# Later places for the last gate/up block, another unit order for the mixer's output product, and query transposes inside the query product

## What is computed

```python
# first block
h = rms_norm(x, mix_norm_g)
x = x + concat(y_pool, y_dn) @ w_mix_out          # y_dn: gated delta net, 8 heads of 128
q = (rms_norm(x, xa_norm_g) @ w_xq)               # 4 heads of 512
k, v = split(rms_norm(mem, mem_norm_g) @ w_xkv)
x = x + softmax(q @ k.T * 512**-0.5) @ v @ w_xo
x = x + (silu(causal_dwconv(h @ w_gate)) * (h @ w_up)) @ w_down     # width 5632
# second block
...
f = square(relu(h @ w_up)) @ w_down               # width 8192
# beside both: mod = silu(c) @ w_ada + b_ada, 24 pieces of 512 columns
```

## Time and profile before

| | |
|---|---|
| median of 3 runs | 2915.92 us (2914.46 to 2915.98) |
| the profiled execution's own time | 2910.81 us |
| its span | 2909.0 us |
| TensorE busy | 2801.5 us, 96% of the span |
| DVE, ACT busy | 1768.6 us (61%), 1313.5 us (45%) |
| mean granted clock of TensorE | 0.978 |
| chain that ended last, share by engine | PE 93%, DVE 4%, ACT 2%, issue 1% |

### The profile page before, as it was taken

The page is one execution under the profiler, slowest core; times in us unless marked ns, Lnnn a source line. Parts: engine busy times, 40 slices in busy tenths (PEclk is TensorE's granted clock), DMA queues, the critical chain, the costliest instruction groups (busy, mean ns, idle before and its releaser), DMA issues.

```text
span 2909.0 us, 35765 instructions
## 1 busy us (share of the span) xinstructions
PE 2801.5 (96%) x13510; PEld 2383.5 (82%) x13510; DVE 1768.6 (61%) x2028; ACT 1313.5 (45%) x1658; POOL 172.1 (6%) x132
## 2 busy tenths in 40 slices
PE   8998989999999999999999989998989999999998
PEld 8998968888878888788888889876778787887886
DVE  4466557776557887765555564454774655744445
ACT  5454234454434545434444454344454344344443
POOL 0001620000000000000000002630000000000000
PEclk9999989999999999999999999998999999999999
DMA  8453028887647777775555556450555765855553
GB/s 281 149 173 115 1 103 284 279 279 266 234 148 253 276 275 263 274 253 195 192 183 203 188 181 201 162 185 1 170 194 186 263 219 204 275 190 172 194 185 122
DMA packets 293265, 579.59 MB, mean 199 GB/s; under 512 B 9168, under 2 KB 46192, under 8 KB 292112
## 3 DMA queue, kind: packets, MB, share of 16 engines
q1 hardware_dynamic: 291296, 566.08, 57.6%
q0 software_dynamic: 1120, 8.57, 0.8%
q10 hardware_dynamic: 720, 3.15, 0.3%
HBM read 575.66 MB, written 2.10 MB: 199 GB/s over the span
## 4 chain that ended last, share of the span: by engine, by line
PE 93%; DVE 4%; ACT 2%; issue 1%; DMA 0%; POOL 0%; DVEq 0%; SPq 0%; ACTq 0%
PE GP L866 28%; PE GP L868 27%; PE GP L867 27%; PE TA L842 2%; PE TB L473 2%; PE TB L842 1%; PE GP L459 1%; PE TB L885 1%; PE TA L1213 1%; DVE wlo L1749 0%; DVE ada_acc L1737 0%; DVE small L550 0%; PE TA L1069 0%; PE GP L1069 0%; PE GP L1059 0%
## 5 line engine op out<-in xcount | busy, mean ns | idle before, releaser
L1749 DVE TENSOR_TENSOR wlo<-raw,whi 128x1024 fp32r<-128x1024 f32 (+2 forms) x904 | 1082.1, 1213 | 777.7 <-ACT whi L1289 766.1
L1289 ACT CAST whi<-raw 128x1024 fp32r<-128x1024 f32 (+2 forms) x904 | 920.7, 1029 | 1152.4 <-PE GP L868 1065.6
L866 PE MATMUL GP<-whi,hhi 128*128 128x512 f32 (+2 forms) x1792 | 691.6, 386 | 9.8 <-DVE wlo L1749 6.7
L867 PE MATMUL GP<-wlo,hhi 128*128 128x512 f32 (+2 forms) x1792 | 683.2, 381 | 0.0
L868 PE MATMUL GP<-whi,hlo 128*128 128x512 f32 (+2 forms) x1792 | 683.1, 381 | 0.0
L866 PEld LDWEIGHTS GP<-whi,hhi 128*128 128x128 f32 x1792 | 340.0, 190 | 62.1 <-issue 10.0
L868 PEld LDWEIGHTS GP<-whi,hlo 128*128 128x128 f32 x1792 | 339.4, 189 | 52.6
L867 PEld LDWEIGHTS GP<-wlo,hhi 128*128 128x128 f32 x1792 | 339.7, 190 | 51.6 <-issue 1.0
L866 PE MATMUL GP<-whi,bhi 128*128 128x512 f32 x704 | 276.7, 393 | 0.2 <-DVE blo L1809 0.2
L1737 DVE SCALAR_TENSOR_TENSOR ada_acc<-raw,csig,ada_acc 128x512 f32<-128x512 f32 x360 | 270.2, 750 | 10.2
L868 PE MATMUL GP<-whi,blo 128*128 128x512 f32 x704 | 274.4, 390 | 0.0
(11 more groups left out here) (413 smaller groups left out, 2660.1 us busy)
## 6 DMA issues: line engine op xcount, KB each, us to landing
raw<-in_w_up SPq DMA_DIRECT2D x108, 1024.0 KB, 5.4
raw<-in_w_down SPq DMA_DIRECT2D x108, 1024.0 KB, 5.1
raw<-in_w_ada SPq DMA_DIRECT2D x96, 1024.0 KB, 5.2
raw<-in_w_gate SPq DMA_DIRECT2D x44, 1024.0 KB, 5.2
raw<-in_w_in SPq DMA_DIRECT2D x48, 856.0 KB, 4.7
raw<-in_w_xkv SPq DMA_DIRECT2D x32, 1024.0 KB, 5.6
raw<-in_w_in SPq DMA_DIRECT2D x24, 1024.0 KB, 4.9
raw<-in_w_in SPq DMA_DIRECT2D x24, 864.0 KB, 4.6
```

The lines of the kernel that those rows point to most:

```text
L866: pe.matmul(o, ahi[:, kt, t], whi[r][:, k, 0:q.width], start=first, stop=False)
L867: pe.matmul(o, ahi[:, kt, t], wlo[r][:, k, 0:q.width], start=False, stop=False)
L1289: nc.scalar.copy(whi[(2 * g + s) % NRING][:, :, 0:q.width], raw[j % NSLOT][:, 2 * s:2 * s + 2, 0:q.width])\
L1749: TTo(wlo[r][:, :, 0:q.width], raw[j % NSLOT][:, 2 * s:2 * s + 2, 0:q.width], whi[r][:, :, 0:q.width].bitcast(F32), ALU.subtract).then_inc ...
```

## The change

1. **Gate/up.** The steps on the last block leave the hook ahead of the next third unit and go behind it (hook 3 of the next iteration, or of the following down product for the last iteration), on ACT and DVE, in `ffn1a`, `ffn1b` and `up20` to `up23`. To have a first iteration that differs, `down1a`, `ffn1b` and the `up2`/`down2` phases are written out with `head`. In `down22` they stand ahead of `gate_column` and `gate_copy`, which are in the same hook.
2. **`mix_out`.** The list of units becomes (block, unit) = 00, 01, 10, 11, 02, 03, 12, 13, and the four "a" loads stand behind the last four units. `rank` is a unit's place in it and takes the place of b * units + u. `out_upper` and the subtraction (`out_lower`) go behind the split of the fourth unit.
3. **Queries.** Three of the four groups are transposed inside `xq`, after its seventh, eleventh and fifteenth unit, all through `TA`; ACT copies each after it has split two more units. The fourth stays behind the product and no longer waits for `ada_read`.

```diff
+        if name == "mix_out":
+            g.sort(key=lambda x: (x[2] // 2, x[1], x[2]))
+        self.rank = {x[1:]: i for i, x in enumerate(g)}
         for i, x in enumerate(g):
             self.seq.append(x)
-            if ada and name == "ffn1a":
-                if 2 <= i < 6:
-                    self.seq.append(("a", 0, i - 2))
+            if ada and name in ("ffn1a", "mix_out"):
+                if 0 <= i - (4 if name == "mix_out" else 2) < 4:
+                    self.seq.append(("a", 0, i - (4 if name == "mix_out" else 2)))
...
-            return q.sub0 + it * q.subs + (b + 1) * 2 * q.units
+            return q.sub0 + it * q.subs + (q.rank[b, q.units - 1] + 1) * 2
...
+                    for b, u in q.rank:
+                        if u == 0:
+                            pe.wait_ge(S(f"evac{b % 2}"), it * (q.nb // 2) + (q.ev0 + b // 2 + 1))
+                        if b == 0:
+                            pe.wait_ge(*ready(u))
+                        for s in range(2):
+                            pos = q.seq.index(("g", b, u))
+
+                            pe.wait_ge(S("unit_used"), it * (2 * len(q.seq)) + 2 * (q.unit0 + pos) + s + 1 + CREDIT)
+                            r = (q.rank[b, u] * 2 + s) % NRING
...
+            def query_turn(g):
+                pe.wait_ge(S(f"evac{g % 2}"), 2 + PH["xq"].ev0 + g // 2)
+                if g == 0:
+                    pe.wait_ge(S("kx_c"), 8)
+                else:
+                    pe.wait_ge(*N("qx", "c", g))
+                for f in range(4):
+                    for h in range(NH):
+                        c = (4 * g + f) * P
+                        m = turn(TA[:, f * T + h * P:f * T + h * P + P], kv[:, h, c:c + P])
+                m.then_inc(N("qx", "t")[0], 1)
+
             product(PH["xq"], hhi, hlo, lambda u: (S("norm_lo"), 16 + 2 * u + 2),
-                    first=lambda: pe.wait_ge(S("norm_lo"), 24), points={unit_of(k): lambda k=k: key_turn(k) for k in range(4)})
-            for e in range(2):
-                pe.wait_ge(S(f"evac{e}"), 1 + PH["xq"].ev1)
-            pe.wait_ge(S("ada_read"), 1 + PH["xq"].ada1)
-            pe.wait_ge(S("kx_c"), 8)
-            turn_in(pe, turn, "qx", kv, 0, 0)
+                    first=lambda: pe.wait_ge(S("norm_lo"), 24), points={unit_of(k): lambda k=k: key_turn(k) for k in range(4)} |
+                    {unit_of(v_): lambda g=g: query_turn(g) for g, v_ in enumerate((6, 10, 14))})
+            query_turn(3)
...
-            out_upper(0)
-            out_upper(1)
...
+            phase(PH["mix_out"], hooked({3: lambda: (out_upper(0), out_upper(1)), 6: lambda: raw_square(1, (0,)), 7: lambda: raw_square(1, (1,)), 11: lambda: raw_root(1)},
...
+            def query_copy(g):
+                act.wait_ge(*N("qx", "t", g + 1))
+                nc.scalar.copy(qTx[:, 4 * g:4 * g + 4, :], v(TA, T)).then_inc(N("qx", "c")[0], 1)
+
+            phase(PH["xq"], hooked({2 + k: lambda k=k: key_copy(k) for k in range(4)} | {v_ + 2: lambda g=g: query_copy(g) for g, v_ in enumerate((6, 10, 14))},
+                                   store(PH["xq"], kv, scale=2)), peel=True)
+            query_copy(3)
...
-                return {q.units + LEAD: [evac(0)], 2 * q.units: [gate], 2 * q.units + LEAD: [evac(1), up]}
-
-            phase(PH["ffn1a"], ffn1(PH["ffn1a"], 0), head={3: [lambda it: raw_square(3)],
-                                                           4: [lambda it: (raw_upper(3, 6), raw_upper(3, 7), raw_root(3))]})
-            phase(PH["down1a"], {})
-            phase(PH["ffn1b"], ffn1(PH["ffn1b"], 6))
+                return {3: [lambda it: None if isinstance(it, int) and it == 0 else up(it - 1)], q.units + LEAD: [evac(0)],
+                        2 * q.units: [gate], 2 * q.units + LEAD: [evac(1)]}, lambda it: up(q.n - 1)
+
+            hooks, rest = ffn1(PH["ffn1a"], 0)
+            phase(PH["ffn1a"], hooks, head={3: [lambda it: raw_square(3)], 4: [lambda it: (raw_upper(3, 6), raw_upper(3, 7), raw_root(3))]})
+            phase(PH["down1a"], {}, head={3: [rest]})
+            hooks, rest = ffn1(PH["ffn1b"], 6)
+            phase(PH["ffn1b"], hooks, head={3: []})
...
-                return {q.units + LEAD: [evac(0)], 2 * q.units: [square(0)], 2 * q.units + LEAD: [evac(1), square(1)]}
+                return {3: [lambda it: it and square(1)(it - 1)], q.units + LEAD: [evac(0)], 2 * q.units: [square(0)],
+                        2 * q.units + LEAD: [evac(1)]}, square(1)
...
+                hooks, rest = up2(PH[f"up2{s}"], s)
+                phase(PH[f"up2{s}"], hooks, head={3: [] if s else [lambda it: (second_upper(1, 6), second_upper(1, 7))]})
+                last = [lambda it, rest=rest: it or rest(1)]
+                phase(PH[f"down2{s}"], {3: last + [lambda it: it and post_block(1, 1)], 7: [lambda it: post_block(1, 2 * it)],
                                         8: [lambda it: root_table() if it else None]} if s == 3 else {},
-                      peel=(s == 3), head={3 + i: [lambda it, i=i: gate_copy(1, i)] for i in range(4)} if s == 2 else {})
+                      peel=(s == 3), head=joined({3: last} if s < 3 else {}, {3 + i: [lambda it, i=i: gate_copy(1, i)] for i in range(4)} if s == 2 else {}))
...
-                return {(b + 1) * q.units + LEAD: [hook(b)] for b in range(q.nb)}
+                return {q.rank[b, q.units - 1] + 1 + LEAD: [hook(b)] for b in range(q.nb)}
...
-            for hf in range(NH):
-                t = slice(hf * P, hf * P + P)
-                dve.wait_ge(S("dn_hi"), hf + 1)
-                TTo(hlo[:, 8:16, t], AB[0][hf], hhi[:, 8:16, t].bitcast(F32), ALU.subtract).then_inc(S("dn_lo"), 1)
-
-            phase(PH["mix_out"], hooked({9: lambda: raw_mean(1), 12: lambda: raw_scale(1)},
+            def out_lower():
+                for hf in range(NH):
+                    t = slice(hf * P, hf * P + P)
+                    dve.wait_ge(S("dn_hi"), hf + 1)
+                    TTo(hlo[:, 8:16, t], AB[0][hf], hhi[:, 8:16, t].bitcast(F32), ALU.subtract).then_inc(S("dn_lo"), 1)
+
+            phase(PH["mix_out"], hooked({3: out_lower, 9: lambda: raw_mean(1), 12: lambda: raw_scale(1)},
...
-                return {2 * q.units: [gate], 2 * q.units + LEAD: [up]}
-
-            phase(PH["ffn1a"], ffn1(PH["ffn1a"], 0), links=2,
+                return {3: [lambda it: None if isinstance(it, int) and it == 0 else up(it - 1)], 2 * q.units: [gate]}, lambda it: up(q.n - 1)
+
+            hooks, rest = ffn1(PH["ffn1a"], 0)
+            phase(PH["ffn1a"], hooks, links=2,
                   head={3: [lambda it: raw_mean(3)], 4: [lambda it: (raw_lower(3, 6), raw_lower(3, 7), raw_scale(3))]})
-            phase(PH["down1a"], add_to_x(PH["down1a"]))
-            phase(PH["ffn1b"], ffn1(PH["ffn1b"], 6), links=2)
+            phase(PH["down1a"], add_to_x(PH["down1a"]), head={3: [rest]})
+            hooks, rest = ffn1(PH["ffn1b"], 6)
+            phase(PH["ffn1b"], hooks, links=2, head={3: []})
...
-                return {2 * q.units: [low(0)], 2 * q.units + LEAD: [low(1)]}
+                return {3: [lambda it: it and low(1)(it - 1)], 2 * q.units: [low(0)]}, low(1)
...
-                    hooks |= {4: [lambda it: it and gated(1, 1)], 8: [lambda it: gated(1, 2 * it)]}
-                phase(PH[f"down2{s}"], hooks, peel=(s == 3), head={3 + i: [lambda it, i=i: gate_column(1, 80, i)] for i in range(4)} if s == 2 else {})
+                    hooks |= {3: last, 4: [lambda it: it and gated(1, 1)], 8: [lambda it: gated(1, 2 * it)]}
+                head = {3 + i: [lambda it, i=i: gate_column(1, 80, i)] for i in range(4)} if s == 2 else {}
+                if s < 3:
+                    head[3] = last + head.get(3, [])
+                phase(PH[f"down2{s}"], hooks, peel=(s == 3), head=head)
             post_mean(1)
             TTo(o3[:, 0, c3], o3[:, 0, c3], gpb[1][:, c3], ALU.mult)
```

More of the change, by code:

```diff
@@ new lines, in iteration @@
+                    for b, u in q.rank:
[7 more added lines that the diff above has]
+                            r = (q.rank[b, u] * 2 + s) % NRING
+                            for k in range(2):
+                                kt = u * UK + 2 * s + k
+                                first, last = kt == 0, kt == q.units * UK - 1
+                                for h in range(NH):
+                                    t = slice(h * P, h * P + P)
+                                    o = GP[:, 2 * (b % 2) + h, 0:q.width]
+                                    pe.matmul(o, ahi[:, kt, t], whi[r][:, k, 0:q.width], start=first, stop=False)
+                                    pe.matmul(o, ahi[:, kt, t], wlo[r][:, k, 0:q.width], start=False, stop=False)
+                                    m = pe.matmul(o, alo[:, kt, t], whi[r][:, k, 0:q.width], start=False, stop=last)
+                            m.then_inc(S("mm_done"), 1)
+                        if mid and b % 2 == 1 and u == 1:
+                            mid(it)
+                        if late and b == 0 and u == 0:
```

(11 more changed lines are left out.)

53 lines of the change are left out of this document (5 added, 48 removed).

## The result

The changed kernel takes **2890.03 us**, the median of 4 runs (2889.56 to 2892.27), beside 2915.95 us (2914.46 to 2916.55) for the kernel before on the same chip: 25.9 us less, a ratio of 0.991 with a 95% interval of 0.9896 to 0.9923. The forecast was 2893.4 us, so 3.4 us of the gain were not in it, and the time lies at the lower end of the range.

What follows compares the result with a forecast made beforehand. TensorE bounds the kernel, busy 2801.5 of 2909.0 us, so only its idle time and the half clock behind stalls could be gained. 12.1 + 1.4 + 8.3 + 0.7 = 22.5 us off 2915.9 gave 2893.4 us, range 2890 to 2901.

Steps and rivals of the forecast that it cites:

- the 1.6 us wait for `dg`: In down22 TensorE waits up to 1.6 us for dg; 1.4 us to be gained, 0.6 as lower bound.
- rival 4: Inner iteration boundaries: moved steps ahead of the fourth unit cause 13 stalls of 4 us, giving 2945; chance 0.03.
- rival 2: Crowded "a" loads in mix_out: TensorE stalls once per iteration, 4 us each, giving 2901.4; chance 0.1.
- Rival 3: Three down products: the wait only moves, as something else holds the third unit, giving 2901.6; chance 0.07.
- the price of `down1a`, `down20`, `down21`: Stalls of 2.66, 2.18 and 2.48 us go, with 1.6 us of half clock each: 12.1 us gained.
- the queries: Score products start 3.4 us earlier, three groups inside xq add 2.65: net 0.7 us gained, between 1.0 gained and 0.9 lost.
- rival 1: Half clock in the score products, all else as forecast: 1.6 us more, 2895.0; chance 0.2.
- an idle time of 1.88 us was not followed by one: Query part: that idle time brought no half clock, one of 2.18 did; used to weigh half clock in the score products.
- the step from the profiled execution to the median: Whole kernel: the median lies 5.1 us above the profiled 2910.8, so 22.5 is taken from 2915.9.
- `mix_out`'s term: In mix_out the 6.72 us stall and 1.6 of half clock go: 8.3 us gained, between 6.7 and 8.4.
- its spread of 1.5 us: Run-to-run spread of the whole kernel, 2914.5 to 2916.0, allowed for in the lower end of the range, 2890.

Runs made afterwards that it cites:

- e8: Kernel before with the four "a" loads of down1a, down20 and down21 put behind the third to sixth unit, last block unmoved; 2902.51 us, ratio 0.9958.
- e9: Kernel before, its order kept, with unused matmuls filling TensorE's four stalls (27 in mix_out, 11, 9 and 10 in down1a, down20, down21); 2906.09 us, ratio 0.9974.
- e7: Kernel after plus ten unused matmuls in the two idle times ahead of the score products (six and four); 2889.15 us, ratio 0.9916 to the kernel before.
- e4: Kernel before with only the query part: three of the four groups transposed inside xq; 2916.84 us, ratio 1.0009.
- e6: Kernel after with its query part undone, all four groups behind the product again; 2890.43 us, ratio 0.9913 to the kernel before.
- the two looks: Two more profiled executions of the unchanged kernel before; 2916.11 and 2917.21 us.
- e1: Kernel before, run and profiled again without edit; 2915.39 us, median of 11 runs, ratio 0.9997; profiled at 2910.6 us.
- e2: Kernel before with only the gate/up part: the last block's steps moved behind the third unit; 2898.45 us, ratio 0.9942.
- e3: Kernel before with only the mix_out part: units and "a" loads reordered, hhi and hlo steps behind the fourth unit's split; 2902.27 us, ratio 0.9959.
- e11: Kernel before, unchanged, profiled once more as the first of two further looks; execution of 2916.11 us.
- e12: Kernel before, unchanged, profiled once more as the second of two further looks; execution of 2917.21 us.
- e5: Kernel after, unchanged, run again on a second chip beside the kernel before; 2891.22 us, ratio 0.992.
- e10: Kernel after with unused matmuls in five idle times of TensorE: 6, 4, 17, 33 and 49; 2885.26 us, ratio 0.9898 to the kernel before.

## Why the prediction was right and wrong

The program is cut here at matmuls that are the same in every trace (the first of a product or of its second iteration, or the first behind transposes); us between them, the forecast's change last. `down1a` and `down20` are first iterations; their second ones are in the row below each:

| stretch | before, 2910.8 | before, 2916.1 | after, 2889.6 | forecast |
|---|---|---|---|---|
| start to `mix_out` | 402.59 | 401.56 | 402.21 | |
| `mix_out` | 105.56 | 103.96 | 94.45 | -8.3 |
| `xkva`, `xkvb` | 181.63 | 181.63 | 181.63 | |
| `xq`, attention | 139.62 | 142.57 | 142.00 | -0.7 |
| `xo`, `ffn1a` | 369.81 | 369.73 | 369.83 | |
| `down1a` | 71.40 | 71.69 | 67.09 | -4.3 |
| `ffn1b` | 298.34 | 298.32 | 298.34 | |
| `down1b` to `w_in2b` | 252.16 | 252.68 | 253.09 | |
| first matmuls of 31 columns | 27.37 | 29.03 | 29.00 | |
| on to `down20` | 414.09 | 416.79 | 413.92 | |
| `down20` | 43.08 | 43.08 | 39.03 | -3.8 |
| on to `down21` | 140.54 | 140.53 | 140.53 | |
| `down21`, `up22` | 183.94 | 183.92 | 179.56 | -4.1 |
| `down22` to the end | 278.87 | 278.81 | 277.12 | -1.4 |
| span | 2909.0 | 2914.3 | 2887.8 | -22.5 |

**Right: where the time goes.** The four stalls and the 1.6 us wait for `dg` are gone, the clock is 1.00 behind them, and nothing took their place at the inner boundaries (rival 4: `ffn1a` and `ffn1b` take what they took) or in `mix_out`'s second half (rival 2: no wait, at 364 GB/s). Rival 3 falls too: with the queue of two steps gone, no `wlo` is late in any of the three, and e8 got nearly there by moving the "a" loads alone. The Trainium skill's limit (DMA: Bandwidth & Descriptors, Specifications: about 358 GB/s for one core) is passed by this row as well.

**Right: the price of `down1a`, `down20`, `down21`.** -4.31, -4.05 and -4.4 us against -4.3, -3.8 and -4.1. e9 measured the half clock behind these three stalls by itself, at 1.4 to 1.6 us.

**Wrong in its inside: the queries.** Counted from the store, the score products start 2.9 us earlier, where 3.4 were forecast, since the fourth group runs at half clock; the three groups cost what they should (`xq` and the way to the first score product take 99.69 us instead of 99.86); and rival 1 came, the half clock in the fourth group and the score products, whose cause e7 showed. The prediction held that "an idle time of 1.88 us was not followed by one"; that was so in the one execution it had, and not in most of the others. Against the short execution of before the part loses 2.4 us, against the long ones it gains 0.6, since in those the old code has more half clock itself; that this comes to about the 0.7 forecast is luck. The times show no gain: e4 lost 0 to 5 us, and e6 lies 0.8 us below the kernel after, less than can be told apart.

**Wrong: the step from the profiled execution to the median.** The prediction said that the median of the runs lies 5.1 us above that execution, and carried this over as a constant: 2915.9 - 22.5. It is no constant. The two short profiles of before ran at 5 us below the median, the two looks 1 to 2 us above it; the profiles of the kernel after lay 0.5 and 2.7 us below theirs. On the short executions the sum looks good: 2910.8 - 22.5 = 2888.3, and 2889.56 and 2888.56 were measured. That is partly luck: between the first and the third column `mix_out` gives 11.1 us and not 8.3, as the short execution begins it at half clock, the query part loses 2.4 instead of gaining 0.7, and the code that the change does not touch takes 2.0 more. The typical execution of before, the long one, has 5.3 us more; its stretches at half clock are longer or more, with TensorE busy in them for 107 us instead of 94. The 5.3 us are 2.95 in the query part, 1.7 and 2.7 at and behind the matmuls of 31 columns, 0.8 in the norm and `down1a`, and 2.6 less up to the end of `mix_out`. Read against it, the parts that the change touches give 9.5 + 0.6 + 4.6 + 4.1 + 4.4 + 1.7 = 24.8 us and the untouched ones another 1.7, against 25.9 by the medians. So the 3.4 us that the forecast was short are 2.3 in its terms and 1.7 in untouched code, less 0.6 between these two executions and the medians.

**Wrong: the size of `mix_out`'s term.** The mechanism was right in this term, its price was not: 8.3 us forecast, with 8.4 as the upper bound, and 9.5 measured against the long execution. Of the 2.3 us between 24.8 and 22.5, 1.2 are this one: in the long execution the clock stays at 0.52 behind the stall for 14 matmuls, which cost 5.79 - 14 x 0.228 = 2.6 us, not for the 8 and 1.6 us of the earlier trace rows; e9, which fills the stall, gets 2.6 us back there. The other four stretches of the sum add 0.3 each, and the queries take 0.1 off. So the price of half clock was taken at the shortest length that it had, for the one place with the longest idle time. The range had too little room as well: its spread of 1.5 us came from three runs, and the eleven of e1 spread over 8.0. So the median came out at the very edge of it. What stays open is the remaining 1.7 us in untouched code: the fewer places at half clock in the kernel after may belong to its timing, or may be chance. The other traces speak against a part of the change that owns them: the stretch of the first 31-column matmuls takes 27.4 or 29.0 us and the one up to `down20` 414 or 417, in all four combinations (short and long in e2 and e6, long and short in e7, short and short in e9, long and long in e4). How often each length comes these runs cannot tell, and the interval of the gain (22 to 30 us) is wider than what is sought.

## What to carry to other kernels

Before costing a stall, look for what stands ahead of the late step in its engine's queue; here the last block's steps and an ada step of 2.8 us stood there, and moving either away was worth 12 us or more. Add to each stall the half clock behind it (here 1.4 to 1.6 us behind one of 2 to 3 us, 2.6 behind one of 6.7 in a typical execution), and where a wait cannot go, matmuls that nothing uses in it are worth a try: 57 of them in the kernel before took 8 us off, 109 in the kernel after 5. And do not forecast a median from one profiled execution by a constant: profile the kernel before two or three times, and take the one whose time is nearest to the median as the base of the sum.

## What the runs showed of the hardware

- Idle times of 2.2 to 2.7 us were followed by 2.9 to 3.4 us of busy TensorE at the 1.2 GHz level in every trace that has them unfilled (before, e1, e3, e4, e11, e12), and half clock also came with two of 1.5 and 1.2 us that have eight transposes between them (0.55 over 7.64 us; after, e4, e5). One of 1.88 or 1.91 us was in six traces and was not in three. Filled with matmuls, the stalls and the pair were not (e7, e9, e10).
- The clock also fell without any idle time: 64 matmuls of 31 columns each took 8.29 us in one execution and 10.71 in another, and the product behind them began at half clock in both (12 matmuls in 4.69 us at 0.50, 8 in 3.04 us at 0.51), with no idle time of TensorE above 0.2 us in the 30 us before.
- The executions of the kernel before that count in a ratio range over 12 us (2908.97 to 2920.9), and the long ones have the lower mean clock (0.974 to 0.975 against 0.978). The Trainium skill says of the matmuls at a kernel's start that the number of slow ones varies between runs of the same kernel (TensorE: Matmul & The Clock Gate, Part 1). The traces show the same behind a stall: in `mix_out` 8 matmuls were slow in one execution and 14 in another.
